# A two-layer retention and attention trunk on one core: the first layer's values as Strassen's seven block products, with token sums moved to GpSimd

## The reference

```
h = rms_norm(x, gain) * (1 + scale) + shift          # scale, shift from the vector c
proj = h @ w_in                                       # 1024 x 6144
q, k, v, g = split(proj, [1024, 2048, 4096])          # v and g are 2048 wide
q, k = rotary(q, positions), rotary(k, positions)     # 4 heads of 256
y = retention(q, k, v, gammas)                        # chunked, with decay
x = x + g1 * ((silu(g) * rms_norm(y)) @ w_out)
x = x + g2 * (square(relu(modulate(x) @ w1)) @ w2)
```

## Time and profile before

| | |
|---|---|
| median of three runs | 2925.73 us (2925.51 to 2925.77) |
| profiled execution, its own time | 2919.89 us |
| its span, first to last instruction | 2918.3 us |
| granted TensorE clock, mean | 0.997 |
| keys end, values start (TensorE) | 225 us |
| values end, gates start | 400 us |

### The profile page before, as it was taken

The page is one execution under the profiler, slowest core; times in us unless marked ns, Lnnn a source line. Parts: engine busy times, 40 slices in busy tenths (PEclk is TensorE's granted clock), DMA queues, the critical chain, the costliest instruction groups (busy, mean ns, idle before and its releaser), DMA issues.

```text
span 2918.3 us, 32758 instructions
## 1 busy us (share of the span) xinstructions
PE 2864.9 (98%) x12724; PEld 2310.4 (79%) x12724; DVE 1829.6 (63%) x2261; ACT 1045.2 (36%) x1341; POOL 338.2 (12%) x486
## 2 busy tenths in 40 slices
PE   6999999999999999999999999999999999999999
PEld 5888888777777888888888787866767888888887
DVE  8865567555558777686765254245454877767673
ACT  5211233322234333333335334344244433333331
POOL 0000000100001000111120010132031100011110
PEclk9999999999999999999999999999999999999999
DMA  7675556743312544754413323465252254475431
GB/s 246 228 256 202 188 178 210 275 158 116 105 44 97 173 159 157 258 179 138 138 44 116 116 81 130 141 147 121 69 120 79 98 173 159 159 266 172 135 137 58
DMA packets 193139, 439.58 MB, mean 151 GB/s; under 512 B 13105, under 2 KB 83172, under 8 KB 192996
## 3 DMA queue, kind: packets, MB, share of 16 engines
q0 software_dynamic: 61616, 222.34, 22.9%
q1 hardware_dynamic: 131380, 215.27, 22.1%
HBM read 314.09 MB, written 123.34 MB: 150 GB/s over the span
## 4 chain that ended last, share of the span: by engine, by line
PE 94%; DVE 3%; ACT 2%; issue 1%; DMA 0%; POOL 0%; DVEq 0%; ACTq 0%; POOLq 0%
PE ps L2706 8%; PE ps L2707 8%; PE ps L2708 8%; PE ps L2879 6%; PE ps L2877 6%; PE ps L2875 6%; PE ps L3007 4%; PE ps L2502 4%; PE ps L2498 4%; PE ps L2501 4%; PE ps L2458 3%; PE ps L2464 3%; PE ps L2461 3%; PE ps L2632 3%; PE ps L2636 3%; PE ps L2635 3%
## 5 line engine op out<-in xcount | busy, mean ns | idle before, releaser
L2875 PE MATMUL ps<-z_hi,w_hi 128*128 128x512 f32 x768 | 298.8, 389 | 0.0
L2877 PE MATMUL ps<-z_lo,w_hi 128*128 128x512 f32 x768 | 298.8, 389 | 0.0
L2879 PE MATMUL ps<-z_hi,w_lo 128*128 128x512 f32 x768 | 298.8, 389 | 0.0
L2706 PE MATMUL ps<-h_hi,w_hi 128*128 128x512 f32 x576 | 224.4, 390 | 0.0
L2708 PE MATMUL ps<-h_hi,w_lo 128*128 128x512 f32 x576 | 224.1, 389 | 0.0
L2707 PE MATMUL ps<-h_lo,w_hi 128*128 128x512 f32 x576 | 224.1, 389 | 0.0
L2498 PE MATMUL ps<-z_hi,w_hi 128*128 128x512 f32 x512 | 203.5, 398 | 0.0
L2502 PE MATMUL ps<-z_hi,w_lo 128*128 128x512 f32 x512 | 199.4, 390 | 0.0
L2501 PE MATMUL ps<-z_lo,w_hi 128*128 128x512 f32 x512 | 199.2, 389 | 0.0
L1577 DVE TENSOR_TENSOR w_lo<-w_raw,w_hi 128x2048 fp32r<-128x2048 f32 x52 | 118.9, 2287 | 121.3 <-ACT w_hi L1036 121.3
L1905 DVE SCALAR_TENSOR_TENSOR xT<-ps,ada,xT 128x512 f32<-128x512 f32 x128 | 93.9, 748 | 147.4 <-PE ps L2502 147.4
(11 more groups left out here) (398 smaller groups left out, 6573.4 us busy)
## 6 DMA issues: line engine op xcount, KB each, us to landing
t_s<-misc POOLq DMA_DIRECT2D x28, 1792.0 KB, 6.9
misc<-t_s POOLq DMA_DIRECT2D x98, 512.0 KB, 4.2
misc<-w_ada SPq DMA_DIRECT2D x84, 512.0 KB, 6.8
w_raw<-w_mlp_in SPq DMA_DIRECT2D x32, 1024.0 KB, 5.7
w_raw<-ret_w_in SPq DMA_DIRECT2D x24, 1024.0 KB, 6.7
x_s<-xT SPq DMA_DIRECT2D x12, 1024.0 KB, 7.4
xT<-x_s SPq DMA_DIRECT2D x12, 1024.0 KB, 11.1
a_bufs<-w_mlp_out SPq DMA_DIRECT2D x12, 1024.0 KB, 22.6
```

What stands on the lines that cost most here:

```text
L2706: MM(out, hi, b_hi[:, k, :], start=k == 0 and i in (0, 1, 3), stop=False, skip_group_check=True)
L2875: MM(bank[at + m], hi, ring_b(z_hi, slot)[:, cols], start=first and i not in (2, 4, 5), stop=False, skip_group_check=True)
L2877: MM(bank[at + m], hi, ring_b(z_lo, slot)[:, cols], start=False, stop=False, skip_group_check=True)
L2879: mm = MM(bank[at + m], lo, ring_b(z_hi, slot)[:, cols], start=False, stop=last, skip_group_check=True)
```

## The change

The values are made by Strassen's scheme too. The 1024 tokens, the 1024 rows of the weights and the 1024 columns of a group are halved each; the 2048 columns make two groups (g = 0, 1). Seven products of 512 tokens x 512 x 512 replace eight, each of 4 token tiles x 4 k x 3 = 48 instructions: `v_product(0)` to `v_product(13)`. Products 2, 3, 4 and 6 of a group use the sums of token blocks that the gates use, so these must be ready earlier; GpSimd now makes them, with the same ten operations, between the spills of key trips 1 to 3. The x that they overwrite is saved at the start of the SP queue's list rather than behind the keys.

Products 2, 3, 4, 5 of a group use sums of weight blocks: VectorE makes the four of group 0 (three of them in the last key trip), GpSimd those of group 1. The weight blocks are held in `w_raw`, in two rows of `misc` (two of the vector tiles' buffers) and in `low_tiles`, so the ring of vector tiles has two buffers from tile 28 on (`ADA_WIDE`). Products that are part of several results are copied from PSUM by ScalarE (`v_keep`, 32 copies) and added by VectorE (`v_add`, 24 operations of 128x512, one operand in PSUM); eight 1 MB spills take the place of sixteen of 512 KB. The vector tiles of chunks 5 to 9 are spread over new places between these steps.

The diff, cut to its core:

```diff
-        ADA_WIDE = 64
+        ADA_WIDE = 28
...
+        v_raw = [w_raw[:, i, :].rearrange("p (k n) -> p k n", n=HALF) for i in range(2)] + \
+            [v_rows(misc[:, 3:5, :]), v_rows(low_tiles[:])]
+        v_slots = [v_rows(stage[:, 4:6, :]), xT[quarter(0, 1)]]
+        V11, V12, V21, V22 = range(4)
+        V_OPERAND = (V11, V12, V11, V22, V21, V12, V11)
+        V_SUM = {3: 1, 4: 2, 2: 3, 5: 4}
+        V_T = {2: 1, 3: 0, 4: 2, 6: 3}
...
+            ada_loads(2, 0, 4)
...
+            ada_loads(2, 4, 8)
+            for i in range(1, 3):
...
+                    key_pair(2 * i + 2 + j)
+                    ada_loads(2 + i, 4 * j, 4 * j + 4)
+            def load_v(g, role, block):
+                m, j = block // 2, block % 2
+                place = v_place(g, role)
+                sp.dma_start(v_raw[place], half_pair(ret_w_in, j, 2048 + 1024 * g + 512 * m)).then_inc(v_loaded[place], 16)
+            load_v(0, V22, V22)
+            sp.wait_ge(lo_done, 7)
+            load_v(0, V11, V11)
+            ada_loads(5, 0, 4)
+            sp.wait_ge(lo_done, 8)
+            load_v(0, V12, V12)
+            ada_load(5, 4)
+            sp.wait_ge(ada_acc_done, 28)
+            load_v(0, V21, V21)
+            ada_loads(5, 5, 8)
+            ada_loads(6, 0, 2)
+            sp.wait_ge(v_sum_done, v_summed(0, 4))
+            sp.wait_ge(v_split_lo, v_split(2))
+            load_v(0, V11, V22)
+            ada_loads(6, 2, 4)
+            sp.wait_ge(v_split_lo, v_split(3))
+            load_v(1, V11, V11)
+            ada_loads(6, 4, 6)
+            sp.wait_ge(v_split_lo, v_split(4))
+            load_v(1, V12, V12)
+            ada_loads(6, 6, 8)
+            sp.wait_ge(v_split_lo, v_split(5))
+            load_v(1, V21, V21)
+            ada_loads(7, 0, 2)
+            sp.wait_ge(v_split_lo, v_split(6))
+            load_v(1, V22, V22)
+            ada_loads(7, 2, 8)
+            ada_loads(8, 0, 2)
+            sp.wait_ge(v_sum_done, v_summed(1, 4))
+            sp.wait_ge(v_split_lo, v_split(9))
+            load_v(1, V11, V22)
+            ada_loads(8, 2, 6)
...
+            ada_loads(9, 0, 8)
...
+            T_OPS = [(i, n) for i in range(4) for n in range(2 if i in (1, 3) else 3)]
+            def gate_t_sum(i, n):
+                out = xT[(quarter(0, 0), quarter(1, 1), quarter(1, 0), quarter(0, 1))[i]]
+                plus = quarter(*((1, 0), (1, 1), (1, 1), (0, 1))[i])
+                minus = (quarter(0, 0), quarter(0, 0), quarter(1, 0), quarter(1, 1))[i]
+                done = t_summed(0, (0, 3, 5, 8)[i])
+                pool.wait_ge(const_ready, 6)
+                if n or i in (1, 3):
+                    pool.wait_ge(in_sum_done, done + n)
+                if n == 0:
+                    first = xT[minus] if i in (1, 3) else h_hi[minus].bitcast(F32)
+                    ins = nc.gpsimd.tensor_tensor(out, h_hi[plus].bitcast(F32), first, ALU.subtract)
+                elif n == 1:
+                    ins = nc.gpsimd.tensor_tensor(out, out, h_lo[plus].bitcast(F32), ALU.add)
+                else:
+                    ins = nc.gpsimd.tensor_tensor(out, out, h_lo[minus].bitcast(F32), ALU.subtract)
+                ins.then_inc(in_sum_done, 1)
+            def gate_t_sums(first, last):
+                for op in T_OPS[first:last]:
+                    gate_t_sum(*op)
+            def spill_keys(i, first, last):
+                for j in range(first, last):
+                    spill(j, qk_s[i * 4 + j:i * 4 + j + 1].rearrange("a p n -> p (a n)"), rot_done, i * 2 + (j // 2 + 1))
+            spill_keys(0, 0, 4)
+            spill_keys(1, 0, 4)
+            pool.wait_ge(h_lo_done, 16)
+            for n in range(4):
+                pool.wait_ge(x_moved[n], 16)
+            gate_t_sums(0, 4)
+            spill_keys(2, 0, 2)
+            gate_t_sums(4, 6)
+            spill_keys(2, 2, 4)
+            gate_t_sums(6, 9)
+            spill_keys(3, 0, 2)
+            gate_t_sums(9, 10)
+            spill_keys(3, 2, 4)
+            def spill_product(g, m, hf, what, waited, value):
+                pool.wait_ge(waited, value)
+                at = v_slot(g, what)
...
+            def v_block_sum(out, a, b, op):
+                pool.wait_ge(const_ready, 6)
+                nc.gpsimd.tensor_tensor(v_raw[out], v_raw[a], v_raw[b], op).then_inc(v_sum_done, 1)
+            spill_product(0, 0, 0, "c11", v_added, v_sum_added(0, 0, 3))
+            spill_product(0, 1, 1, "c22", v_added, v_sum_added(0, 1, 3))
+            a11, a12, a21, a22 = (v_place(1, role) for role in range(4))
+            pool.wait_ge(v_loaded[a21], v_load_count(a21, 2))
+            pool.wait_ge(v_loaded[a22], v_load_count(a22, 3))
+            v_block_sum(a22, a21, a22, ALU.add)
+            spill_product(0, 0, 1, "c12", v_added, v_sum_added(0, 2, 3))
+            pool.wait_ge(v_loaded[a11], v_load_count(a11, 2))
+            pool.wait_ge(v_sum_done, v_summed(1, 1))
+            v_block_sum(a21, a11, a21, ALU.subtract)
+            spill_product(0, 1, 0, "c21", v_kept, v_copied(0, 3, 3))
+            pool.wait_ge(v_split_lo, v_split(7))
+            pool.wait_ge(v_sum_done, v_summed(1, 2))
+            v_block_sum(a11, a22, a11, ALU.subtract)
+            pool.wait_ge(v_split_lo, v_split(8))
+            pool.wait_ge(v_sum_done, v_summed(1, 3))
+            v_block_sum(a12, a12, a11, ALU.subtract)
+            spill_product(1, 0, 0, "c11", v_added, v_sum_added(1, 0, 3))
+            spill_product(1, 1, 1, "c22", v_added, v_sum_added(1, 1, 3))
+            spill_product(1, 0, 1, "c12", v_added, v_sum_added(1, 2, 3))
+            spill_product(1, 1, 0, "c21", v_kept, v_copied(1, 3, 3))
...
-            with act.Fori(1, 4) as i:
+            def v_high(n):
+                g, i = divmod(n, 7)
+                place = v_place(g, V_OPERAND[i])
+                if n == 0:
+                    act.wait_ge(w_begun, 8)
+                elif n == 1:
+                    act.wait_ge(a_full, A_QK + 16)
+                else:
+                    act.wait_ge(v_full, v_ready(n - 2, 3))
+                if i in V_SUM:
+                    act.wait_ge(v_sum_done, v_summed(g, V_SUM[i]))
+                else:
+                    act.wait_ge(v_loaded[place], v_load_count(place, (1 if i < 6 else 2) if g == 0 else (2 if i < 6 else 3)))
+                nc.scalar.activation(v_part(w_hi, n), v_raw[place], ACT.Copy).then_inc(v_split_hi, 1)
...
+            def v_keep(g, n):
+                i, what = ((0, "p1"), (2, "u2"), (3, "p5"), (6, "c21"))[n]
+                at = v_slot(g, what)
+                if (g, n) == (0, 0):
+                    act.wait_ge(rot_done, 8)
+                elif (g, n) == (0, 1):
+                    act.wait_ge(split_lo_done, t_split(0, 3))
+                else:
+                    act.wait_ge(v_spilled[at], v_spill_count(((0, 0, 1, 2), (1, 3, 2, 3))[g][n]))
+                for t in range(4):
+                    act.wait_ge(v_full, v_ready(7 * g + i, t))
+                    nc.scalar.activation(v_slots[at][:, t, :], bank[t + (4 if n == 2 else 0)], ACT.Copy).then_inc(v_kept, 1)
+            v_high(1)
+            gate_t_high(3)
+            v_high(2)
+            gate_t_high(1)
+            v_keep(0, 0)
...
+            v_high(3)
+            v_keep(0, 1)
+            v_high(4)
+            gate_t_high(2)
+            v_keep(0, 2)
+            v_high(5)
+            v_high(6)
+            v_high(7)
+            v_keep(0, 3)
+            v_high(8)
+            v_keep(1, 0)
+            v_high(9)
+            v_high(10)
+            v_keep(1, 1)
+            v_high(11)
+            v_keep(1, 2)
+            v_high(12)
+            v_high(13)
+            gate_high(0, 0)
+            gate_high(0, 1)
+            v_keep(1, 3)
...
+            def v_low(n):
+                g, i = divmod(n, 7)
+                dve.wait_ge(v_split_hi, v_split(n))
+                TT(v_part(w_lo, n), v_raw[v_place(g, V_OPERAND[i])], v_part(w_hi, n).bitcast(F32), ALU.subtract)\
+                    .then_inc(v_split_lo, 1)
+            def v_block_sum(n):
+                if n == 0:
+                    dve.wait_ge(v_loaded[2], v_load_count(2, 1))
+                    dve.wait_ge(v_loaded[3], v_load_count(3, 1))
+                else:
+                    dve.wait_ge(v_sum_done, v_summed(0, n))
+                if n == 1:
+                    dve.wait_ge(v_loaded[0], v_load_count(0, 1))
+                elif n > 1:
+                    dve.wait_ge(v_split_lo, v_split(n - 2))
+                out, a, b, op = ((V22, V21, V22, ALU.add), (V21, V11, V21, ALU.subtract),
+                                 (V11, V22, V11, ALU.subtract), (V12, V12, V11, ALU.subtract))[n]
+                TT(v_raw[out], v_raw[a], v_raw[b], op).then_inc(v_sum_done, 1)
+            def last_trip():
+                prep(W_QK + 7, 1)
+                ada_tiles(5, 0, 5)
+                rotary(12, 0)
+                v_low(0)
+                v_block_sum(0)
+                v_block_sum(1)
```

(143 more changed lines are left out.)

140 lines of the change are left out of this document (61 added, 79 removed).

## The result

The changed kernel takes 2935.06 us (median of 8 runs, 2930.13 to 2938.41) against 2924.20 for the kernel before (8 runs, 2919.77 to 2927.74). The ratio is 1.0039, interval 1.0028 to 1.0051: slower by 11 us, where 14 were forecast. The profiled execution took 2934.75 us, with a span of 2933.2.

A forecast was written before the change was run, and what follows sets the result against it. TensorE, busy for 98% of the span, was taken as the bound. Terms -21.9 - 0.8 + 13.1 + 10.8 + 7.7 + 2.0 + 3.2 = +14.1 us on 2925.7 gave 2939.8 us, range 2908 to 2958.

The forecast's parts named there:

- products, and the old wait: Value stage: 672 products instead of 768 save TensorE 21.9 us, and its 0.8 us wait ahead of the values goes.
- first wait: Key trips, lane sum of chunk 4, near 180 us: TensorE waits 13.1 us for VectorE's late transposing sum.
- second wait: Key trips, lane sum of chunk 5, near 237 us: TensorE waits 10.8 us for late VectorE.
- splits 8 and 9: Values: GpSimd's four block sums of group two delay VectorE's splits 8 and 9; TensorE waits 7.7 us (0 to 10).
- loads: Vector tile loads, with two buffers where there were four: +2 us (0 to 4).
- clock: TensorE runs at half clock after the first and second wait: +3.2 us (0 to 6.4).
- The exclusion: GpSimd's token sums and VectorE's operations on two SBUF inputs take turns; each sum holds VectorE for 4.4 us.
- Rival one: No exclusion between GpSimd and VectorE at these shapes: TensorE waits 1 us or so, time 2905 us; chance 0.13.
- rival two: GpSimd is served only in VectorE's pauses: 9 us of wait, time 2915 us (2908 to 2922); chance 0.15.
- Rival three: Token sums also late for ScalarE, two buffers stop VectorE among tiles: four more waits of 4 us, 2956 us; chance 0.10.

The follow-up runs named there:

- run 1: The changed kernel with its ten token sums on VectorE instead of GpSimd: 2912.76 us, ratio 0.9962 to the kernel before.
- run 2: The kernel before, plain products, with token spill and sums moved into the key trips: sums on GpSimd 2940.54 us (1.0063), on VectorE 2921.55 us (0.9995).
- run 4: The changed kernel with each of GpSimd's ten token sums cut into two halves of 128x1024: 2931.48 us, ratio 1.0030.
- Run 3: The changed kernel with GpSimd's token sums 5 and 6 held back until VectorE's transposing sum of chunk 4 is done: 2933.61 us, ratio 1.0040.
- run 6: The kernel of run 1 with the second group's four block sums moved from GpSimd to VectorE too: 2908.38 us, ratio 0.9955.
- run 7: The kernel of run 6 with value splits 7, 8 and 9 placed ahead of block sums or vector tiles: 2908.39 us, ratio 0.9947.
- run 9: Run 7 with adds and split 10 before chunk 7's eighth tile, its lane columns earlier, splits 11 and 12 before two or three tiles: 2909.93 us, ratio 0.9954.

## Why the prediction was right

By its steps, forecast and measured:

| step | forecast | measured |
|---|---|---|
| products, and the old wait | -22.7 | -22.7 (the account closes with it) |
| first wait | 13.1 | 12.3 |
| second wait | 10.8 | 8.7 |
| splits 8 and 9 | 7.7 | 5.8 |
| loads | 2.0 | 0 of its own |
| clock | 3.2 | 7.0 |
| sum | 14.1 | 11.1 |

The pace of the products is measured too: from 248.5 to 411.8 us, less 5.8 of waits and 4.2 of clock, the 672 take 0.228 us each. That the sum came so near is in part luck: waits and loads were forecast 6.8 us too high and the clock 3.8 too low, and the two errors work against each other.

**The exclusion.** Right in kind and size: 4.1 to 4.4 us for nine of the ten holds and 3.5 for the fourth, whose tile was issued late, behind the lane columns; 4.4 was forecast, from the pair of rows behind the retention. Every sum was issued while VectorE was in an operation, so its row includes its own wait. Counted from that operation's end it is shorter: the split of 144.10 ends at 146.39 and sum 1 at 150.85, the tile of 146.30 at 151.40 and sum 2 at 155.86, 4.46 us both times, where 4.6 were forecast. The prediction gives all of VectorE's operations there two SBUF inputs; the chunk's first tile has one, and it was held too. Runs 1 and 2 show that it is the engine, run 4 that it goes by whole instructions. The rule of the Trainium skill (page SBUF — State Buffer, section SBUF: two separate sides) is that the two lock each other out of a shared pair of ports for a whole instruction. The trace agrees: a half holds 2.1 us in run 4, a whole 4.35. The Trainium skill's page GPSIMD Engine Reference (section 3.1 Elementwise — side-by-side cycle accounting) has 4497 ns for such a sum; the trace agrees to 0.04 us, with the 4.46 us counted from VectorE's end. Rival one (no exclusion) is out, and so is rival two (GpSimd served only in the pauses): the two tiles at 151.51 stood ready in a row, and a sum went ahead of each.

**The two waits.** Right in place and cause. They were forecast 0.8 and 2.1 us too long. Run 3 confirms the step that sums 5 and 6 come between VectorE and its transposing sum: 8.8 forecast, 8.4 measured.

**Splits 8 and 9.** The size was nearly right and the cause only in part. The step put the lateness on four holds. Runs 6 and 7 have none and still show 3 to 5 us of waits in the values, run 9 none there and 5.9 in the gates: by the rows of run 7 it is the ring of two buffers, a tile every 2.7 us or so, with 32 tiles to pass. That is the loads' term, taken as +2 in all. Without GpSimd's sums the kernels gain 13.2 to 17.5 us (ratios of 0.9955 to 0.9940) of the 22.7. In run 7, 3.4 us of the rest are these waits and 1.7 the clock behind them. Another part nobody forecast: TensorE waits for the values' way back from DRAM in the retention, 2.6 to 3.6 us in every kernel with seven products and 1.8 to 1.9 in those with plain ones, and in run 7 1.7 us of clock follow. Rival three named this stop and was given 0.10 because VectorE has 33 us to spare by busy time; its further waits did not come on top of GpSimd's, where TensorE was late itself.

**The clock.** The term that missed by most for its size, 3.2 against 7.0. I took 1.6 us for each long wait, from the pause at 30 us, and nothing for short ones. The two long waits cost 2.9 and 2.5, and that of 4.0 us another 1.7.

## What to carry to other kernels

An idle GpSimd is no free engine for SBUF sums: each held VectorE for nearly its own length, so 22.8 us of VectorE work became some 42 us of standstill, and cutting it up changed little. The same sums in VectorE's own pauses cost nothing, even at 42 of 44 us busy. Where in-order engines hand on a backlog, moving an instruction moves the wait: look for the resource that sets the pace (here, by the rows, two buffers for the tiles) before ordering around it. Versions with all sums on VectorE beat both kernels: 0.994 to 0.9955 of the kernel before, not told apart among themselves; 0.9940 is the lowest.
